# Forget gates in float32 in four strips of TensorE, and the first two projection units taken chunk by chunk

## The reference, cut to what matters

```python
def rmsnorm(x, g):
    xf = x.astype(jnp.float32)
    y = xf * lax.rsqrt(jnp.mean(xf * xf, axis=-1, keepdims=True) + EPS)
    return (y * g.astype(jnp.float32)).astype(x.dtype)

def project(xn, w_in, b_forget, pos):
    y = jnp.einsum('bld,de->ble', xn, w_in)
    offs = np.cumsum(IN_SIZES)[:-1].tolist()
    q_a, k_a, v_a, f_a, q_b, k_b, v_b, g_a, g_b = jnp.split(y, offs, axis=-1)
    ...
    logf = jax.nn.log_sigmoid((f_a + b_forget).astype(jnp.float32))
```

## Time and profile before

| | |
|---|---|
| median of 3 runs | 1680.81 us |
| profiled execution | 1680.76 us |
| its span | 1679.0 us |
| PE busy | 1651.5 us, 98% |
| PE's part of the chain that ended last | 80% |
| DVE, ACT, POOL busy | 1083.5, 775.8, 310.2 us |
| first matmul of the forget gates | 19.39 us |
| first matmul of unit 2, of unit 3 | 47.37, 60.29 us |
| first FoX score matmul | 73.20 us |

### The profile page before, as it was taken

How to read it: one execution, slowest core, us unless ns; L and a number is a source line. 1 busy time by engine, 2 the same in 40 slices (tenths; PEclk the granted TensorE clock), 3 DMA queues, 4 the chain that set the end, 5 groups by cost and what they waited for, 6 DMA issues and landing times.

```text
span 1679.0 us, 27411 instructions
## 1 busy us (share of the span) xinstructions
PE 1651.5 (98%) x9540; PEld 1489.3 (89%) x9540; DVE 1083.5 (65%) x2322; ACT 775.8 (46%) x1630; POOL 310.2 (18%) x438
## 2 busy tenths in 40 slices
PE   8999999999999999999999999999999999999998
PEld 8999999999999988989988899888888888888886
DVE  7556666553999744454445597888877667774744
ACT  6477777765777533352233333222222334443521
POOL 1311111115333211124532230000000000000242
PEclk9999999999999999999999999999999999999999
DMA  5221212231222554563443422444432763444641
GB/s 187 77 61 41 79 47 59 67 110 36 74 57 67 163 179 160 160 210 123 147 140 111 134 85 94 131 144 144 144 131 105 258 220 111 132 149 125 192 163 75
DMA packets 164314, 205.34 MB, mean 122 GB/s; under 512 B 16152, under 2 KB 113240, under 8 KB 164208
## 3 DMA queue, kind: packets, MB, share of 16 engines
q1 hardware_dynamic: 164208, 203.97, 38.0%
HBM read 144.85 MB, written 57.28 MB: 120 GB/s over the span
## 4 chain that ended last, share of the span: by engine, by line
PE 80%; DVE 9%; ACT 4%; issue 4%; POOL 2%; DMA 0%; DVEq 0%; ACTq 0%; SPq 0%; POOLq 0%
PE gb L503 8%; PE gb L3173 6%; PE gb L2290 5%; PE sc L3173 5%; PE gb L2825 4%; PE gb L2661 4%; PE sc L2825 4%; PE tp L3173 4%; PE tp L2825 4%; PE tp L798 3%; PE sc L2449 3%; PE tp L2449 3%; PE gb L930 3%; PE gb L931 2%; PE gb L932 2%
## 5 line engine op out<-in xcount | busy, mean ns | idle before, releaser
L930 PE MATMUL gb<-Xh,wh 128*128 128x384 f32 (+1 forms) x504 | 175.9, 349 | 0.0
L489 POOL TENSOR_TENSOR wl<-raw,wh 128x256 fp32r<-128x256 f32 x168 | 125.0, 775 | 264.2 <-ACT wh L474 175.4
L931 PE MATMUL gb<-Xh,wl 128*128 128x384 f32 (+1 forms) x504 | 170.7, 339 | 0.0
L932 PE MATMUL gb<-Xl,wh 128*128 128x384 f32 (+1 forms) x504 | 170.7, 339 | 0.0
L3297 POOL TENSOR_TENSOR wl<-raw,wh 128x1024 fp32r<-128x1024 f32 x2 | 5.3, 2626 | 559.0 <-ACT wh L3288 559.0
L503 PE MATMUL gb<-Xh,wh 128*128 128x384 f32 (+1 forms) x288 | 103.9, 361 | 0.0
L503 PE MATMUL gb<-Xh,wl 128*128 128x384 f32 (+1 forms) x288 | 97.4, 338 | 0.0
L503 PE MATMUL gb<-Xl,wh 128*128 128x384 f32 (+1 forms) x288 | 97.3, 338 | 0.0
L930 PEld LDWEIGHTS gb<-Xh,wh 128*128 128x128 f32 x504 | 95.0, 189 | 0.1
L931 PEld LDWEIGHTS gb<-Xh,wl 128*128 128x128 f32 x504 | 95.0, 188 | 0.0
L932 PEld LDWEIGHTS gb<-Xl,wh 128*128 128x128 f32 x504 | 94.8, 188 | 0.0
(11 more groups left out here) (548 smaller groups left out, 4777.4 us busy)
## 6 DMA issues: line engine op xcount, KB each, us to landing
zr<-u_scr SPq DMA_DIRECT2D x91, 256.0 KB, 3.0
raw<-in_w_in SPq DMA_DIRECT2D x70, 256.0 KB, 3.2
u_scr<-ustore SPq DMA_DIRECT2D x26, 576.0 KB, 3.6
u_scr<-ustore SPq DMA_DIRECT2D x13, 768.0 KB, 3.2
sig_scr<-sig SPq DMA_DIRECT2D x16, 576.0 KB, 3.1
raw<-in_w_up SPq DMA_DIRECT2D x36, 256.0 KB, 4.4
kc<-in_cache_fox_k SPq DMA_DIRECT2D x8, 1024.0 KB, 5.6
vc<-in_cache_fox_v SPq DMA_DIRECT2D x8, 1024.0 KB, 7.6
```

What stands on the lines that cost most here:

```text
L489: nc.gpsimd.tensor_tensor(wl[U.slot][:, q], raw[U.slot][:, q], wh[U.slot][:, q].bitcast(F32), ALU.subtract).then_inc(w_lo if x == 3 else w ...
L930: nc.tensor.matmul(gb[c][:, 0:x1 - x0], wh[U.slot][:, ws], Xh3[:, k, x0:x1], start=(k == 0), stop=False)
L931: nc.tensor.matmul(gb[c][:, 0:x1 - x0], wl[U.slot][:, ws], Xh3[:, k, x0:x1], start=False, stop=False)
L932: last = nc.tensor.matmul(gb[c][:, 0:x1 - x0], wh[U.slot][:, ws], Xl3[:, k, x0:x1], start=False, stop=(k == KT - 1))
```

## The change

The gate weights are no longer split. They are kept in float32, 32 columns (8 used, 24 zero) for each of the 8 inner blocks; ACT copies the first four blocks, POOL the others. `gates(c)` multiplies four inner blocks in four 32-column strips of the array, whose results go to four strips of 32 partitions of the bank: 4 sets (2 groups of blocks, high and low part of x) of 4 float32 matmuls. ACT copies the whole bank to SBUF (`f_sum_act`), and a float32 product with `f_pick`, a 128 x 8 matrix of ones and zeros, sums the strips (`f_pick_pe`). `lf_dve_z` then adds only the bias.

Units 1 and 2 are taken in turn by `unit(n, c)`; the order of PE's first nine results is `FIRST`. Unit 2's weights are loaded ahead of tiles 8 and 9 and cast between `high(4)` and `high(5)`. Unit 2's chunk 2 goes to the bank `po`. Several ACT and DVE steps stand in other places, and the cast of unit 3's weights waits for unit 1's last chunk. The scratch tile `junk` is now a part of `nC`.

```diff
+        f_sums, f_pick, f_tmp = nB, sig[:, 0:8], sig[:, 16:64]
+        fw = sig[:, 64:320]
...
-            load(sp, Unit(U_F), cols_of(I["w_in"], COL_F))
+            load(sp, Unit(U_F), f_parts())
             rows_in(4)
-            load(sp, Unit(1), cols_of(I["w_in"], COL_QA))
-            rows_in(5, 6, 7, 8, 9)
+            load(sp, Unit(1), parts_of(1))
+            rows_in(5, 6, 7)
+            load(sp, Unit(2), parts_of(2))
+            rows_in(8, 9)
...
             root(2)
+            f_sum_act(act, 0)
             square(6)
             square(7)
             root(3)
             high(4)
+            hi_second(act)
+            high(5)
+            q_keep(act, 1, 0, 0)
             square(8)
...
+        FIRST = [(0, 0), (1, 0), (2, 0), (0, 1), (1, 1), (0, 2), (2, 1), (1, 2), (2, 2)]
...
-                for k in range(KT):
+                for k0 in (0, 4):
                     for j, x_ in enumerate((Xh3, Xl3)):
-                        last = nc.tensor.matmul(fbank[c][:, 0:b - a], fw3[:, k, :], x_[:, k, a:b],
-                                                start=(k == 0 and j == 0), stop=(k == KT - 1 and j == 1))
...
+                        for g in range(4):
+                            last = nc.tensor.matmul(fbank[c][32 * g:32 * g + 32, 0:b - a], fw3[:, k0 + g, :],
+                                                    x_[:, k0 + g, a:b].bitcast(F32),
+                                                    start=(k0 == 0 and j == 0), stop=(k0 == 4 and j == 1))
...
+        def f_pick_pe(c):
+            a, b = CHUNK_ALL[c]
+            pe.wait_ge(f_zero, 3)
+            pe.wait_ge(f_summed, c + 1)
+            nc.tensor.matmul(fbank[c][0:8, 0:b - a], f_pick, f_sums[:, a:b], start=True, stop=True).then_inc(f_picked, 1)
...
+            def unit(n, c, between=()):
...
+                    pe.wait_ge(w_lo, n + 1)
...
+                elif n == 2:
+                    pe.wait_ge(bank_free[c], 2)
...
+            tiles_split(4)
+            gates(0)
+            unit(1, 0, [lambda: None, lambda: turn(4), lambda: turn(5)])
+            f_pick_pe(0)
+            unit(2, 0, [lambda: None, lambda: turn(6)])
+            tiles_split(7)
+            gates(1)
+            unit(1, 1, [lambda: turn(7), lambda: None, lambda: turn(8)])
+            f_pick_pe(1)
+            turn(9)
+            unit(2, 1, [lambda: None, gates_2])
+            f_pick_pe(2)
+            unit(1, 2)
+            unit(2, 2)
...
             q_keep(act, 1, 2, 0)
+            hi(act, Unit(3), used=first_done(1, 2))
             act.wait_ge(lf_chain, 3)
             nc.scalar.activation(ll[:, :], lw_[:, :], ACT.Ln).then_inc(lf_act, 1)
-            hi(act, Unit(3))
```

More of the change, by code:

```diff
@@ L599, in norm_act, with f_rows, f_copy_act, f_copy_pool @@
             high(4)
+            hi_second(act)
+            high(5)
+            q_keep(act, 1, 0, 0)
             square(8)
-            high(5)
+            high(6)
             square(9)
-            high(6)
             root(4)
-            f_low_act(act, 0)
             high(7)
+            f_sum_act(act, 1)
             high(8)
-            f_low_act(act, 1)
+            q_keep(act, 1, 1, 0)
             high(9)
-        def f_hi_act(act):
+            f_sum_act(act, 2)
+        def f_rows(k0):
+            return fw3[:, k0:k0 + 4, 0:8], raw[0][:, :].rearrange("p (k n) -> p k n", k=KT)[:, k0:k0 + 4, 0:8]
+        def f_copy_act(act):
             act.wait_ge(raw_full[0], 32)
             act.wait_ge(f_zero, 1)
-            nc.scalar.activation(fw3[:, :, 0:8], raw[0][:, :].rearrange("p (k n) -> p k n", k=KT)[:, :, 0:8],
-                                 ACT.Copy).then_inc(w_hi, 1)
-        def f_lo_pool(pool):
-            pool.wait_ge(w_hi, 1)
-            nc.gpsimd.tensor_tensor(fw3[:, :, 32:40], raw[0][:, :].rearrange("p (k n) -> p k n", k=KT)[:, :, 0:8],
-                                    fw3[:, :, 0:8].bitcast(F32), ALU.subtract).then_inc(w_lo, 1)
+            to, src = f_rows(0)
+            nc.scalar.activation(to, src, ACT.Copy).then_inc(w_hi, 1)
+        def f_copy_pool(pool):
+            pool.wait_ge(raw_full[0], 32)
+            pool.wait_ge(f_zero, 1)
+            pool.wait_ge(w_hi, 1)
+            to, src = f_rows(4)
+            nc.gpsimd.tensor_copy(to, src).then_inc(w_lo, 1)
+        def f_pick_dve(v):
+            four_id = ident[:, :].rearrange("p (g r) -> p g r", g=4)
+            two = f_tmp[:, 0:16].rearrange("p (g r) -> p g r", g=2)
+            nc.vector.tensor_tensor(two, four_id[:, 0:2, 0:8], four_id[:, 2:4, 0:8], ALU.add).then_inc(f_zero, 1)
+            v.wait_ge(f_zero, 2)
+            nc.vector.tensor_tensor(f_pick, f_tmp[:, 0:8], f_tmp[:, 8:16], ALU.add).then_inc(f_zero, 1)
         def hi_second(act):
@@ L727, in turn, with gates @@
                     last.then_inc(tp_full, 1)
-            def gates(c, between=()):
+            def gates(c):
                 a, b = CHUNK_ALL[c]
@@ L770, in norm_pe, with tiles_split, gates_2 @@
             in_motion(20)
-            turns = (((), (4, 5, 6)), ((7,), (8, 9)), ((), ()))
-            for c in range(3):
+            def tiles_split(n):
                 for h in range(2):
-                    pe.wait_ge(tp_free[h], 3 * c + 4)
-                gates(c, [lambda t=t: turn(t) for t in turns[c][0]])
-                first(c, [lambda t=t: turn(t) for t in turns[c][1]])
+                    pe.wait_ge(tp_free[h], n)
+            def gates_2():
+                tiles_split(10)
+                gates(2)
+            tiles_split(4)
[12 more added lines that the diff above has]
+            unit(2, 2)
         class Count:
@@ L3452, in _ @@
             norm_sp(sp)
-            load(sp, Unit(2), parts_of(2))
             load(sp, Unit(3), parts_of(3))
@@ L3507, in _ @@
             norm_act(act)
-            hi_second(act)
-            for c in range(2):
-                q_keep(act, 1, c, 0)
-            f_low_act(act, 2)
             lf_act_(act)
@@ L3614, in _ @@
             lf_dve(v)
-            for c in range(2):
-                k_keep(v, 2, c, 0)
             q_split_dve(v, 0)
             q_zero_dve(v, 0, DH)
-            k_keep(v, 2, 2, 0)
             k_split_dve(v, 0)
@@ L3773, in _ @@
             norm_pe(pe)
-            for n in (2, 3):
-                for c in range(3):
-                    gemm(pe, Unit(n), c, CHUNK_ALL[c])
+            for c in range(3):
+                gemm(pe, Unit(3), c, CHUNK_ALL[c])
             pe.wait_ge(cst_r, 2)
```

53 lines of the change are left out of this document (30 added, 23 removed).

## The result

The changed kernel takes 1694.54 us, the median of 4 runs (1694.11 to 1695.47), against 1680.72 us for the kernel before in the same session (4 runs). The ratio is 1.0084, with an interval from 1.0067 to 1.0101: it is slower by 13.8 us. The prediction said slower, but by 5.3 us, and its range ended at 1689.0. So its sign was right, and its size was wrong by 8.5 us.

A forecast was written before the change was run, and what follows sets the result against it. PE was taken to bound the kernel (busy 98%, 80% of the chain). +0.2 + 2.9 - 1.1 + 3.6 = +5.6 us, less 0.3 for overlap, gave +5.3 on 1680.81: 1686.1 us, range 1683.3 to 1689.0.

The forecast's parts named there:

- Gates: Forget-gate products on PE, float32 in four strips: sets 0.67 us apart, 3.0 us for 400 columns, +0.2 us in all.
- rival B: Gate products: the strips overlap less, 1.4 us more over the three chunks, 1687.5 us; chance 0.06.
- strips one by one (C): Gate products: the four strips run one after another, 10.7 us a chunk, +23 us, 1709 us; chance 0.01.
- two passes (D): Float32 gates and sums: two passes do where four were counted, +0.4 us, 1681.2 us; chance 0.03.
- Summing products: One new float32 product per chunk on PE, taken at the upper bound: +2.9 us, at least +1.9.
- Old wait: PE's 1.1 us wait at chunk 1's gates, for DVE's low half of tile 6, goes: -1.1 us.
- New waits: PE waits 2.4 us before unit 2 chunk 0, 0.5 before its chunk 1, 0.7 before unit 3: +3.6 us.
- Rival A: Before unit 2: the DVE and ACT loop closes before PE comes, no 2.4 us wait, 1683.7 us; chance 0.13.
- Rival E: After the long wait before unit 2: PE's clock slows, costing 1 to 3 us, up to 1689 us; chance 0.05.
- Edits at nothing: Other edits, such as load order, scratch tile and the forget chain starting 12.2 us later, were priced at no cost.

The follow-up runs named there:

- run 3: The kernel before, with one wait added on SP so that unit 5's load is issued only when unit 3's products are done: 1685.86 us, ratio 1.0029.
- run 1: The changed kernel, with SP's load of unit 5's weights issued ahead of the store of the running sums: 1686.87 us, ratio 1.0037.
- run 2: The changed kernel, load left late, with ACT's cast and POOL's low half of unit 5 moved behind the second FoX step: 1686.65 us, ratio 1.0035.
- run 4: The kernel before, with only the float32 gates in four strips and the summing products, all else in the old order: 1684.40 us, ratio 1.0023.
- run 7: The changed kernel, with ACT's copy of chunk 0's gate sums behind squares 6 and 7: 1691.20 us, ratio 1.0055.
- run 5: The changed order of units, loads and casts, with the old gates and no summing products: 1690.68 us, ratio 1.0055.
- run 6: The changed kernel, with 16 unread transposes of the identity put into PE's wait ahead of unit 2's first chunk: 1690.24 us, ratio 1.0053.

## Why the prediction was wrong

**Gates**, predicted +0.2: right. Sets at 0.67 us; 2.82 us in all for 400 columns and 2.72 for 384 (38.48 to 41.20), and 0.1 us more on the neighbours at each edge. No overlap was lost (rival B), and strips one by one (C) or two passes (D) fell as well.

**Summing products**, predicted +2.9: right within a tenth or two, though below the upper bound that was taken for each. They hold PE 0.83 (28.56 to 31.51, less the wait of 2.12), 0.74 and 0.74 us, and some 0.5 us on the neighbours.

**Old wait**, -1.1: gone. By distances between starts it had cost 1.3 (the earlier trace rows show the idle part alone).

**New waits**, predicted 2.4, 0.5 and 0.7: the first two were right, at 2.12 and 0.5 (the turn and the wait before unit 2's second chunk take 1.29 us where a turn takes 0.79), and the third was 0.3 (0.4 by starts). The releaser was the one named, ACT's copy behind DVE's bias add at 30.22, and the loop is the one described: DVE idles 2.20 us before the seventh and eighth tiles' inverse (forecast 2.2), the bias add comes 0.6 us earlier than forecast and POOL's low half of unit 2 ends at 30.59 (31.4). These four terms make 0.2 + 2.8 - 1.3 + 3.0 = 4.7 us; the first score stood 4.6 us late with the clock left out, against the forecast's 5.3. Rival A asked for a bias add done by 28.9, which did not come.

**Rival E**, the clock, had been given 0.05 and 1 to 3 us. It was there, for 1.5 us, in this execution, and again behind the second wait. It should have had more than that: its condition was the forecast's own wait.

**The step that failed is "Edits at nothing"**, in the sentence that the late forget chain is "hidden by under 1 us, and if that cover is gone the softmax is late by what is missing, where a transpose two steps on has slack". The running sums themselves did come in time: DVE's first reader runs at 80.01, 0.7 us behind the first score, as in the kernel before. But the step followed the late chain to its own reader alone. It did not ask what stands behind the store and the loads in SP's queue, which is the load of unit 5; who waits for that, which is ACT's cast ahead of the softmax; and what stands behind the cast on POOL, which is the tail that PE needs. And the transpose had next to no slack: where it waits, it starts 0.28 us behind the start of the MEMSETs (89.36 to 89.64, and 81.55 to 81.83 in run 3); before, it was 0.45 (78.35 to 78.80), so 0.17 us to spare. Nothing of this needed the changed kernel. The issue of the load at 62.37, right behind `ckb`, the cast at 73.45 and POOL's row of four stood in the trace of before. By the forecast's own numbers the scan ends 12.8 us later, so the load is issued at 75.2, and its cast is due at 78.7, with the first score: 3.5 us for a transfer that took 3.6 us in run 3 and 7.5 in the changed kernel, where the loads of the running sums, 520 KB each, are issued 1.1 us ahead of it (in run 3 they are long done, issued at 61.25; unit 6's load follows in both). That these loads make the difference fits the DMA share of 0.97 but was not tried apart. What the step priced at nothing cost 4.7 us of waiting and 1.6 us of low clock, 6.3 in all. Runs 1 and 2 give back 7.7 and 7.9 by their medians, which hold the first fall of the clock as well, and 6.5 and 5.6 behind the first score of their profiled executions; run 3 makes 5.2 of it in the old kernel.

With 4.6 us to the score, 1.5 for the first fall of the clock, 6.3 at the transpose and 1.0 behind, the 13.4 us are accounted for. No version here beats the kernel before.

## What to carry to other kernels

When a step becomes late, list what stands behind its DMA instructions on the issuing queue, and follow each of those loads to the engine that needs it, then to what that engine has queued behind it; the reader of the late data is only one of the victims. A load's slack is the time from its landing to its first use, and it is read by the releaser of that use: a cast that is released by PE has slack, one released by a DMA has none. In an order written by hand, a cast for later goes behind the softmax that is due now.

## What the runs showed of the hardware

The granted clock can fall after a short wait. PE's first wait, for the identity at the start, is left out here. After 1.0 to 1.4 us of PE idle time it fell in none of the profiles (before, runs 4 and 7); after 2.1 us it fell in two (the changed kernel and run 2) and not in a third (run 1), which has the same wait in the same place; after 3.0 us and more it fell each time (five waits of 3.1 to 4.5 us at the transpose, one of 3.0 before unit 2). Matmuls of 400 columns then stand 0.33 us apart in place of 0.18, the 1.2 GHz level in place of 2.4. One fall cost 1.5 or 1.6 us in five cases and 2.8 in three (before unit 2 in run 5, at the transpose in runs 6 and 7). With the early wait of 2.1 us it seems to come in some executions and not in others: that may be a part of the 3.7 us between the fastest and the slowest execution of run 2, but only profiled executions show the clock.

The Trainium skill, TensorE: Matmul & The Clock Gate, Why this matters for your kernels, warns of idle gaps between bursts of matmuls. The traces agree with the warning; its price here is the one above, and it already holds for a wait of 2.1 us.

The low half of unit 4's weights on POOL took 6.85 us in place of 3.87, while DVE ran the steps of the forget chain and the scan beside it. It moved no wait of PE, and its cause was not tried.
